# Router scores with the tokens as TensorE's held operand, and the norm's small term added in ScalarE's root

## The chip, the cores and the metric

The kernel runs on one core of a Trainium2 chip. The metric is the time of one execution on the device in microseconds, as the median of several runs. One more execution was recorded by the hardware profiler; all views below are of that one. The engines are PE (TensorE; PEld is its loading of the held operand), DVE (VectorE), ACT (ScalarE), POOL (GpSimd) and SP, which issues most of the transfers.

## What is computed

Two transformer blocks, one after the other, on 256 tokens of width 1024 in float32. Each ends its sublayers with a layer norm, and each has one sublayer of routed experts. The parts that the change touches are these:

```python
def _layer_norm(x, g, b):
    mu = jnp.mean(xf, axis=-1, keepdims=True)
    var = jnp.mean(jnp.square(xf - mu), axis=-1, keepdims=True)
    y = (xf - mu) * lax.rsqrt(var + LN_EPS) * g + b
...
def _grouped_moe(x, router_w, router_b, w1, w3, w2):   # first block, 16 experts
    scores = jax.nn.sigmoid((xt @ router_w).astype(jnp.float32))
    biased = scores + router_b.astype(jnp.float32)
    # two experts of one group per token, gates from scores, then the chosen experts
...
```

The second block has 8 experts of width 3584 and takes the two largest of `h @ moe_w_router` for each token; its gates are a softmax over these two.

## The kernel before

The tokens are kept as two tiles of 128 tokens (`TT = 2`), their width as eight blocks of 128 (`KT = 8`). `hT` holds the normed tokens turned round: width on the partitions, 256 tokens along the free axis. Every engine has one program, written out by hand, and semaphores tie them together. The work outside the experts is a list of units. TensorE emits a unit into a bank of PSUM (`emit`), ScalarE takes it out again (`save_unit`), and `proj_ready` and `proj_saved` count them. The bank is chosen by the unit's number, odd or even (`psB2` and `psB3`).

**The router.** After the norm ahead of it, TensorE turns the tokens (L1386, into `hT` by ScalarE at L1960), keeps itself busy with products that nobody reads (L1364), and then makes the scores by two units. Unit "held" (L1278) holds the router weights (16 or 8 columns) and moves all 256 tokens past them, eight products in all, one for each block of the width; ScalarE copies the result, experts on the partitions, to `route_rows` (L1979). Unit "back" (L1282) turns it round with two small transposes, and ScalarE saves it as scores with tokens on the partitions (L1981), through a sigmoid in the first block, which needs another table (ACT_TABLE_LOAD). VectorE then ranks and chooses (L2589 to L2602), TensorE counts the tokens of each expert with a triangular matrix (unit "cum", L1302), and VectorE turns the counts into places (L2622, L2608). In the first block a unit of 30 small products for a later stage ("compressed bias", L1325) stands on TensorE between the scores and the count. The experts' tokens are gathered (L1671), turned (L1687) and multiplied with weights that stream in by DMA (L1622; SP issues at L945). Their slots come free as the products use them.

**The norm.** VectorE sums the statistics (L2499), aggregates them to mean and variance in `mvar` (BN_AGGR, L2426), adds 1e-5 to the variance into `veps` (L2427), and asks ScalarE for the root (L1914). Then it takes the reciprocal (L2429) and scales the tokens (L2421). Seven norms do this once for each tile of 128 tokens (`norm_half`, on ScalarE `half_root`), two do it for both tiles at once (`layer_norm` with a source, L2443 to L2447, on ScalarE `root`, L1910). The last norm (L2410) has code of its own and isn't changed. `eps` is a column of the tile `small`, filled at the start.

Of the kernel before, what the change touches and what calls it, by code (L numbers as in the profile page):

```python
# [23 lines left out]
ALU = mybir.AluOpType  # L24
# [167 lines left out]
def two_block_kernel(nc, I, out):  # L192
    ctx = ExitStack()
    with ctx:
# [190 lines left out]
        rows_dram = nc.dram_tensor("bias_rows", (16, 2, ROW_W), F32, kind="Internal").ap()  # L385
        ones = sb("ones", [P, T])
        route = S[:].rearrange("p a b c -> p (a b c)")[:, 0:1000]
        route_rows = S[:].rearrange("p a b c -> p (a b c)")[:, 1024:1024 + T]
        at_slots = Slots(S[:].rearrange("p a b c -> p (a b c)")[:, 1280:1536], 0)
        slot_base, slot_id, gate_of, same_id = (at_slots.get(n) for n in (E2, TT * E2, TT * E2, TT * E2))  # L390
        two_back, back_gate, gate_sum = (at_slots.get(n) for n in (4, 4, TT))
# [218 lines left out]
        residual("mem1 out", I["mem_wo"][0])  # L610
        transposes("ln2 transposed", h, hT, 2)
        route_in = route[:, 0:TT * E1].rearrange("p (a b) -> p a b", a=TT)
        unit("router1", "held", (rw1, E1), route_rows[0:E1])
        unit("router1", "back", (E1,), route_in, ACT.Sigmoid)
        unit("compressed bias", "cb", (), bcmp)
        unit("count1", "cum", (route_gate[:, :, 0:E1], E1), route_count)
        routed("moe1")
# [5 lines left out]
        for i in range(2):  # L623
            transposes(f"ln{3 * i + 3} transposed", h, hT, 3 * i + 3)
            if i == 0:
                w = I["ev_w_in_2"][0]
                c = chunk(kxn(w)[:, :, 512:640], w=128)
                unit("mix2", "tok", (hT, c, KT, 128, 0, 128), ckv)
                c = chunk(kxn(w)[:, :, 1152:1224], w=72)
                unit("mix2", "dup", (hT, c, KT, 72, 0, 1), kiT)  # L630
                unit("mix2", "tok", (hT, c, KT, 72, 64, 8), wi, ACT.Copy, 8.0 ** -0.5)
                project("mix2", "T", hT, w, qiT, 640, 2)
                for j in range(8):
                    unit("indexer", "idx", (j,), idx_act[:, j % 2], ACT.Relu, 0.125)
                project("mix2b", "T", hT, w, qaT, 0, 2)
                project("mix2b", "T", hT, w, qbT, 1224, 2, scale=0.125)
                c = chunk(kxn(w)[:, :, 1736:1992])
                unit("mix2b", "dup", (hT, c, KT, 256, 0, 2), kbT)
                unit("mix2b", "tok", (hT, c, KT, 256, 128, 128), vb)
                for j in (0, 4, 1, 5):  # L640
                    unit("latent queries", "uk", (j,), qlatT[:, j:j + 3:2, :], ACT.Copy, 0.125)
                unit("latent keys", "ctr", (), cT)
                for j in range(4):
                    unit("latent out", "uv", (j,), yT[:, j, :])
                residual("out2", I["ev_w_out_2"][0])
            else:
                w = I["od_w_in_2"][0]
                project("mix3", "T", hT, w, kvcT[:, :, 0:T], 1024, 1)

                def queries(name, j, n):  # L650
                    project(name, "T", hT, w, qcT[:, 2 * j:2 * j + 2 * n, :], COLS * j, n, scale=0.125)

                for br, name in enumerate(("od_w1_k_2", "od_w1_v_2")):
                    if br == 1:
                        queries("mix3 first queries", 0, 1)
                        queries("mix3 second queries", 1, 1)
                    v = I[name][0].rearrange("(j d) c -> d j c", d=64)
                    cs = [chunk([(row, 64, 1024 * k, v[:, 16 * k + 8 * a:16 * k + 8 * a + 8, :]) for row in (0, 64)
                                 for k in range(2)], 16, 128) for a in range(2)]
                    unit(("compressed key parts", "compressed value parts")[br], "hidden", (br, cs), cmp_parts[:, br])  # L660
                c = chunk(kxn(w)[:, :, 1792:1840], w=48)
                unit("mix3 gates", "tok", (hT, c, KT, 48, 0, 48), g3, ACT.Sigmoid)
                own_banks()
                for g in range(2):
                    unit("compress joined", "join", (g,), geluT[:, :, g, 0:N_CMP], ACT.Gelu_apprx_tanh)
                queries("mix3 third queries", 2, 1)
                own_banks()
                unit("compress out", "kc", (), kcT)
                unit("compress out", "vc", (), vc4)
                queries("mix3 last queries", 3, 1)  # L670
                for c0, kd, vd in ((1280, ksT, vs), (1536, kwT, vw)):
                    c = chunk(kxn(w)[:, :, c0:c0 + 256])
                    unit("mix3 keys", "dup", (hT, c, KT, 256, 0, 2), kd)
                    unit("mix3 keys", "tok", (hT, c, KT, 256, 128, 128), vd)
                for t in range(TT):
                    adds.append(("compressed logits", None, t, None))
                for par in range(2):
                    unit("compressed probs", "pctr", (par,), pcT[:, par])
                residual("out3", I["od_w_out_2"][0])
            transposes(f"ln{3 * i + 4} transposed", h, hT, 3 * i + 4)  # L680
            project(f"xa{i} queries", "T", hT, I["xa_w_q_2"][i], mqT, 0, 2, scale=128.0 ** -0.5)
            residual(f"xa{i} out", I["xa_w_o_2"][i], 4)
            transposes(f"ln{3 * i + 5} transposed", h, hT, 3 * i + 5)
            if i == 0:
                experts("dense", FF_DENSE // COLS)
                in_part[0] = 3
            else:
                unit("router2", "held", (rw2, E2), route_rows[0:E2])
                unit("router2", "back", (E2,), route[:, 0:TT * E2].rearrange("p (a b) -> p a b", a=TT))
                unit("count2", "cum", (route_gate[:, :, 0:E2], E2), route_count[:, :, 0:E2])  # L690
                routed("moe2")

# [476 lines left out]
        def _(pe):  # L1169
# [35 lines left out]
            def turned_pair(u, k):  # L1205

                if u in behind_norm and k % 2 == 0:
                    pe.wait_ge(proj_saved, behind_norm[u] + 1 + k // 2)

            def emit(u):  # L1210
# [58 lines left out]
                elif kind == "tr":  # L1269
                    src, j0, _ = args  # L1270
                    for j in range(2):
                        for t in range(TT):
                            last = nc.tensor.transpose(bank[:, T * j + P * t:T * j + P * t + P],
                                                       src[:, t, P * (j0 + j):P * (j0 + j) + P], eye)
                elif kind == "held":
                    for k in range(KT):
                        turned_pair(u, k)
                        last = mm(bank[0:args[1], 0:T], args[0][:, k, :], hT[:, k, :], start=(k == 0), stop=(k == KT - 1))  # L1278
                elif kind == "back":
                    pe.wait_ge(proj_saved, u)  # L1280
                    for t in range(TT):
                        last = nc.tensor.transpose(bank[:, args[0] * t:args[0] * t + args[0]],  # L1282
                                                   route_rows[0:args[0], P * t:P * t + P], eye[0:args[0], 0:args[0]])
                elif kind == "ptr":
                    for k in range(2):
                        nc.tensor.transpose(bank[:, 32 * k:32 * k + 32], pe_rows[0:32, k], eye[0:32, 0:32])
# [608 lines left out]
        def _(act):  # L1895
# [11 lines left out]

            def root():
                request()
                answer(ap_(std, veps, ACT.Sqrt))  # L1910

            def half_root(t):
                request()
                answer(ap_(std[:, t:t + 1], veps[:, t:t + 1], ACT.Sqrt))  # L1914

            highs = [0]

# [35 lines left out]
            def save_unit(u):  # L1953
# [21 lines left out]
                        ins = ap_(dest, pair(bank), func, scale=scale)  # L1975
                    elif kind == "row":
                        ins = ap_(dest, bank[0:16, :], func)
                    elif kind == "held":
                        ins = ap_(dest, bank[0:args[1], 0:T], func)  # L1979
                    elif kind == "back":  # L1980
                        ins = ap_(dest, pair(bank, args[0]), func)  # L1981
                    elif kind == "cum":
                        ins = ap_(dest, pair(bank, args[1]), func, scale=scale)
                    elif kind == "sumsq":
# [352 lines left out]
        def _(dve):  # L2337
# [85 lines left out]

            def norm_half(t):

                do(V.bn_aggr(mvar[:, t, :], stats[:, t].rearrange("p a b -> p (a b)")))  # L2426
                ask(V.tensor_scalar(veps[:, t:t + 1], mvar[:, t, 1:2], EPS, None, ALU.add))  # L2427
                answer()
                do(V.reciprocal(rstd[:, t:t + 1], std[:, t:t + 1]))  # L2429
                for cut in (slice(0, D),) if t == 0 else (slice(0, D // 2), slice(D // 2, D)):  # L2430
                    scale_normed(h, t, cut)

            def layer_norm(src=None, ahead=None, stage=None, behind=None, alpha=None):
# [4 lines left out]
                if src is not None:  # L2438
                    for j in range(D // COLS):
                        ins = sums(src, j)  # L2440
                    do(ins)
                    for t in range(TT):
                        ins = V.bn_aggr(mvar[:, t, :], stats[:, t].rearrange("p a b -> p (a b)"))  # L2443
                    do(ins)
                    ask(V.tensor_scalar(veps, mvar[:, :, 1], EPS, None, ALU.add))
                    answer()
                    do(V.reciprocal(rstd, std))  # L2447
                    for t, cut in ((0, slice(0, D)), (1, slice(0, D // 2)), (1, slice(D // 2, D))):
                        scale_normed(src, t, cut)
# [739 lines left out]
```

## Time and profile before

| | us |
|---|---|
| median of 3 runs | 2262.59 (2260.28 to 2264.58) |
| the profiled execution | 2264.02 |
| its span, from first to last instruction | 2262.2 |
| busy in it: PE, DVE, ACT | 2141.7, 1551.9, 1274.8 |
| mean granted clock of TensorE, as a share of full speed | 0.97 |

The experts take the stretches from about 340 to 580 us and from about 1255 to 2240 us; the rest is attention and projections. In the timelines a row gives the start in us, the length in us, the engine, the line, what is written from what, the shapes, and in brackets for how long the engine had nothing to do and what ended that. A float32 product shows as two records, so eight products are x16. A row of stretches gives the busy time of each engine, then TensorE's granted clock (1.00 is 2.4 GHz, 0.50 is 1.2 GHz), the DMA engines' busy share and GB/s.

### The profile page before, as it was taken

The page shows a single profiled execution, that of the slowest core. Times are in us where ns is not written, and L with a number is a line of the kernel's source. Part 1 is how long each engine was busy: PE and PEld are TensorE (multiplying, and loading weights), DVE is VectorE, ACT ScalarE, POOL GpSimd, SP SyncE. Part 2 cuts the span into 40 slices and gives each one's busy share as a digit, 9 for nine tenths or more (in the row PEclk, how much of TensorE's full clock was granted, in tenths as well). Part 3 has the DMA queues.
Part 4 walks back from the last instruction along what each step waited for, and adds up shares of the span by engine and source line. Part 5 has one row for each costly group of instructions (what it writes and reads, how often), then busy time and mean ns, then how long its engine had stood idle before and what let it go on. Part 6 is the DMA issues. An engine that isn't in the chain of part 4 may idle for free. (4 is left out here: it accounts for less than half of the span.)

```text
span 2262.2 us, 33121 instructions
## 1 busy us (share of the span) xinstructions
PE 2141.7 (95%) x12242; PEld 1718.4 (76%) x12242; DVE 1551.9 (69%) x2217; ACT 1274.8 (56%) x1674; POOL 185.3 (8%) x142
## 2 busy tenths in 40 slices
PE   8998999998988989999999899999999999999996
PEld 8886884443787779997768688888888888888875
DVE  4557651221556686665377798898888888888987
ACT  4555441111334453443364777787777778777774
POOL 2112000000000013340000010001001010101000
PEclk9998998999989999998999899999999999999999
DMA  8640649999552244658212799999999999999994
GB/s 269 184 156 1 196 159 375 416 416 415 180 182 94 84 157 161 203 164 206 82 37 86 287 375 363 378 369 372 369 375 370 374 374 372 375 365 376 367 395 175
DMA packets 293952, 602.56 MB, mean 266 GB/s; under 512 B 17835, under 2 KB 123711, under 8 KB 285520
## 3 DMA queue, kind: packets, MB, share of 16 engines
q1 hardware_dynamic: 285392, 571.56, 69.8%
q0 software_dynamic: 8448, 29.49, 4.0%
q8 instruction: 72, 1.18, 0.2%
q14 instruction: 40, 0.33, 0.0%
HBM read 595.15 MB, written 5.83 MB: 266 GB/s over the span
## 5 line engine op out<-in xcount | busy, mean ns | idle before, releaser
L2099 ACT ACTIVATE arena_rounded<-ring 128x1024 fp32r<-128x1024 f32 x452 | 471.0, 1061 | 114.5 <-DMA ring<-in_moe_w_up_dram 65.0
L2810 DVE TENSOR_TENSOR ring_rounded<-ring,arena_rounded 128x1024 fp32r<-128x1024 f32 x452 | 525.2, 1218 | 12.8 <-ACT arena_rounded L2099 10.5
L1185 PE MATMUL psF<-arena_rounded 128*128 128x512 f32 x896 | 357.9, 399 | 1.5 <-ACT arena_rounded L2121 1.5
L1187 PE MATMUL psF<-arena_rounded 128*128 128x512 f32 x896 | 354.2, 395 | 0.0
L1186 PE MATMUL psF<-ring_rounded,arena_rounded 128*128 128x512 f32 x896 | 353.1, 394 | 0.0
L2371 DVE TENSOR_TENSOR ring_rounded<-ring,ring_rounded 128x2048 fp32r<-128x2048 f32 (+1 forms) x71 | 154.0, 2170 | 162.1 <-ACT ring_rounded L1925 161.9
L1187 PEld LDWEIGHTS psF<-arena_rounded 128*128 128x128 f32 x896 | 168.6, 188 | 39.3
L1185 PEld LDWEIGHTS psF<-arena_rounded 128*128 128x128 f32 x896 | 168.9, 188 | 38.9 <-ACT arena_rounded L2121 1.8
L1186 PEld LDWEIGHTS psF<-ring_rounded,arena_rounded 128*128 128x128 f32 x896 | 168.8, 188 | 37.9
L1186 PE MATMUL psB<-ring_rounded,PT_rounded 128*128 128x512 f32 x448 | 177.7, 397 | 0.0
L1925 ACT ACTIVATE ring_rounded<-ring 128x2048 fp32r<-128x2048 f32 (+1 forms) x71 | 128.6, 1813 | 84.7 <-PE psF L1187 62.7
L1185 PE MATMUL psB<-yT_rounded,ring_rounded 128*128 128x256 f32 x464 | 136.8, 295 | 5.3 <-DVE memT_rounded L2393 4.0
L2099 ACT ACTIVATE mv_rounded<-ring 128x1024 fp32r<-128x1024 f32 x110 | 116.7, 1061 | 38.1 <-DMA ring<-in_moe_w_down_dram 38.0
L1186 PE MATMUL psB<-memT_rounded,ring_rounded 128*128 128x256 f32 x464 | 135.3, 292 | 0.0
L1187 PE MATMUL psB<-yT_rounded,ring_rounded 128*128 128x256 f32 x464 | 135.0, 291 | 0.0
L2099 ACT ACTIVATE memT_rounded<-ring 128x1024 fp32r<-128x1024 f32 x110 | 116.1, 1062 | 31.3 <-DMA ring<-in_moe_w_down_dram 31.2
L2810 DVE TENSOR_TENSOR ring_rounded<-ring,memT_rounded 128x1024 fp32r<-128x1024 f32 x110 | 130.5, 1217 | 2.1 <-ACT memT_rounded L2099 1.4
L2810 DVE TENSOR_TENSOR ring_rounded<-ring,mv_rounded 128x1024 fp32r<-128x1024 f32 x110 | 129.3, 1216 | 0.0
L2815 DVE TENSOR_TENSOR PT_rounded<-psF,PT_rounded 128x512 fp32r<-128x512 f32 x56 | 38.7, 691 | 102.6 <-ACT PT_rounded L2109 102.6
L1187 PE MATMUL psB<-mv_rounded,PT_rounded 128*128 128x512 f32 x260 | 102.6, 395 | 0.0
L1187 PE MATMUL psF<-yT_rounded,ring_rounded 128*128 128x256 f32 x352 | 99.9, 284 | 0.0
L1185 PEld LDWEIGHTS psB<-yT_rounded,ring_rounded 128*128 128x128 f32 x464 | 93.2, 201 | 8.7 <-ACT hT L1960 5.8
(478 smaller groups left out, 4575.5 us busy)
## 6 DMA issues: line engine op xcount, KB each, us to landing
ring<-in_moe_w_gate_dram SPq DMA_DIRECT2D x224, 512.0 KB, 5.7
ring<-in_moe_w_up_dram SPq DMA_DIRECT2D x224, 512.0 KB, 5.7
ring<-in_moe_w_down_dram SPq DMA_DIRECT2D x224, 512.0 KB, 5.4
ring<-in_w_dram SPq DMA_DIRECT2D x48, 1024.0 KB, 16.4
arena<-in_w_dram SPq DMA_DIRECT2D x16, 1024.0 KB, 18.9
ring<-in_w_in_dram SPq DMA_DIRECT2D x14, 1024.0 KB, 5.3
ring<-in_ff_w_gate_dram SPq DMA_DIRECT2D x11, 1024.0 KB, 7.2
ring<-in_ff_w_up_dram SPq DMA_DIRECT2D x11, 1024.0 KB, 9.7
```

Source lines behind the costliest of these rows:

```text
L1185: mm(bank, x1, w1, start=start, stop=False, skip_group_check=open_groups)
L1186: mm(bank, x1, w2, start=False, stop=False, skip_group_check=open_groups)
L1187: return mm(bank, x2, w1, start=False, stop=stop, skip_group_check=open_groups)
L1925: ap_(ring_r[:, hi_slot[c], 0:kt * w].bitcast(R32), ring[:, slot_of[c], 0:kt * w], ACT.Copy)\
L2099: ap_(half_slot(slot, w_hi).bitcast(R32), half_slot(slot, raw_halves), ACT.Copy).then_inc(q["high"], 1)
L2371: V.tensor_tensor(ring_r[:, slot_of[c], 0:kt * w].bitcast(R32), raw, ring_r[:, hi_slot[c], 0:kt * w], ALU.subtract).then_inc(weights_low, 1)
L2810: V.tensor_tensor(half_slot(slot, low_halves).bitcast(R32), half_slot(slot, raw_halves), half_slot(slot, w_hi), ALU.subtract).then_inc(q[" ...
L2815: V.tensor_tensor(hiddenT_lo.bitcast(R32), Z[0][:, :].rearrange("p (f s) -> p f s", f=4), hiddenT_hi, ALU.subtract).then_inc(q["turned_dve ...
```

## The change

The two units of a router become one, "scores". It holds a block of the turned tokens (128 by 128) and moves the router weights (16 or 8 columns) past it: sixteen products, eight for each tile of tokens. The result has tokens on the partitions at once. The copy to `route_rows`, the transposes and their unit are gone. Since there is one unit less, all units between the two routers use the other one of the two banks; their order and waits are the same.

In nine norms the addition of 1e-5 on VectorE is gone (sixteen instructions: fourteen for a tile, two for both); ScalarE's root reads the variance from `mvar` and takes `eps` as its bias, and the aggregate is what asks for it.

```diff
-                elif kind == "held":
-                    for k in range(KT):
-                        turned_pair(u, k)
-                        last = mm(bank[0:args[1], 0:T], args[0][:, k, :], hT[:, k, :], start=(k == 0), stop=(k == KT - 1))
-                elif kind == "back":
-                    pe.wait_ge(proj_saved, u)
+                elif kind == "scores":
+                    w, n = args
                     for t in range(TT):
-                        last = nc.tensor.transpose(bank[:, args[0] * t:args[0] * t + args[0]],
-                                                   route_rows[0:args[0], P * t:P * t + P], eye[0:args[0], 0:args[0]])
+                        for k in range(KT):
+                            if t == 0:
+                                turned_pair(u, k)
+                            last = mm(bank[:, n * t:n * t + n], hT[:, k, P * t:P * t + P], w[:, k, :],
+                                      start=(k == 0), stop=(k == KT - 1))
...
             def half_root(t):
                 request()
-                answer(ap_(std[:, t:t + 1], veps[:, t:t + 1], ACT.Sqrt))
+                answer(ap_(std[:, t:t + 1], mvar[:, t, 1:2], ACT.Sqrt, bias=eps))
...
-                    elif kind == "held":
-                        ins = ap_(dest, bank[0:args[1], 0:T], func)
-                    elif kind == "back":
-                        ins = ap_(dest, pair(bank, args[0]), func)
+                    elif kind == "scores":
+                        ins = ap_(dest, pair(bank, args[1]), func)
...
             def norm_half(t):
 
-                do(V.bn_aggr(mvar[:, t, :], stats[:, t].rearrange("p a b -> p (a b)")))
-                ask(V.tensor_scalar(veps[:, t:t + 1], mvar[:, t, 1:2], EPS, None, ALU.add))
+                ask(V.bn_aggr(mvar[:, t, :], stats[:, t].rearrange("p a b -> p (a b)")))
                 answer()
```

TensorE at the first router, before. `hT` and `small` are the turned tokens and the router weights (here and below the router weights lie in `small`), `tab` and `ohot` are the later stage's bias.

```order
L1386 MATMUL psB<-cw,h 128x128 x8
L1364 MATMUL psF<-cw 128x256 x5
L1278 MATMUL psB<-hT,small 16x256 x8
L1282 MATMUL psB<-cw,S 128x16 x2
L1325 MATMUL psB<-tab,ohot 128x16 x30
L1302 MATMUL psB<-small,cw 128x16 x4
```

The same place after:

```order
L1382 MATMUL psB<-cw,h 128x128 x8
L1360 MATMUL psF<-cw 128x256 x5
L1278 MATMUL psB<-small,hT 128x16 x16
L1321 MATMUL psB<-tab,ohot 128x16 x30
L1298 MATMUL psB<-small,cw 128x16 x4
```

Eight products of 256 columns and two transposes have become sixteen products of 16 columns; the thirty bias products now stand right behind them.

ScalarE at the first router, before:

```order
L1960 ACTIVATE hT<-psB,small 128x256 x8
L1979 ACTIVATE S<-psB 16x256
L1981 ACT_TABLE_LOAD
L1981 ACTIVATE S<-psB 128x32
L2079 ACTIVATE arena<-h 128x2048
```

The same place after:

```order
L1956 ACTIVATE hT<-psB,small 128x256 x8
L1975 ACT_TABLE_LOAD
L1975 ACTIVATE S<-psB 128x32
L2073 ACTIVATE arena<-h 128x2048
L2076 ACTIVATE hT_rounded<-h 128x2048
```

The copy is gone, so the table load now follows the saves of the turned tokens directly.

## Rows read from the trace of the kernel before

**Rows 1.** the page, part 2: busy share of the DMA engines in 40 slices (tenths).
```profile
DMA  8640649999552244658212799999999999999994
```

**Rows 2.** the timeline around the first router: start us, length us, engine, line, what.
```profile
324.57 3.63 PE L1278 MATMUL psB<-hT,small 128*16 128x256 f32 x16
...
328.24 0.37 ACT L1979 ACTIVATE S<-psB 16x256 f32<-16x256 f32 x1 [2.63 <-PE psB L1278]
328.63 1.28 ACT L1981 ACT_TABLE_LOAD   x1
...
328.75 0.26 PE L1282 MATMUL psB<-cw,S 16*128 16x16 f32 x2 [0.55 <-ACT S L1979]
...
328.95 8.95 PE L1325 MATMUL psB<-tab,ohot 33*128 33x16 f32 x60
...
330.21 0.19 DVE L2643 TENSOR_TENSOR S<-S,small 128x32 f32<-128x32 f32 x1 [2.84 <-issue]
...
334.71 0.09 DVE L2602 MEMSET small<- 128x34 f32 x1
...
337.83 1.89 PE L1302 MATMUL psB<-small,cw 128*128 128x16 f32 x8
...
339.98 0.19 DVE L2622 TENSOR_TENSOR small<-small,S 128x32 f32<-128x32 f32 x1 [2.85 <-ACT small L1983]
```

**Rows 3.** the timeline around the second router.
```profile
1245.32 3.62 PE L1278 MATMUL psB<-hT,small 128*8 128x256 f32 x16
...
1248.97 0.37 ACT L1979 ACTIVATE S<-psB 8x256 f32<-8x256 f32 x1 [2.62 <-PE psB L1278]
...
1249.79 0.18 ACT L1981 ACTIVATE S<-psB 128x16 f32<-128x16 f32 x1 [0.44 <-PE psB L1282]
...
1250.07 0.29 DVE L2589 TENSOR_TENSOR S<-S 128x128 f32<-128x128 f32 x1 [1.96 <-ACT S L1981]
...
1252.08 0.38 PE L1302 MATMUL psB<-small,cw 128*128 128x8 f32 x1 [2.33 <-DVE small L2600]
```

**Rows 4.** the timeline of TensorE: two products in the form that the change takes.
```profile
80.32 3.63 PE L1259 MATMUL psB<-small,hT 128*128 128x4 f32 x32
...
646.03 3.74 PE L1259 MATMUL psB<-ring,hT 128*128 128x8 f32 x32
```

**Rows 5.** stretches: from:to us, length, each engine's busy us, TensorE clock, DMA share, GB/s.
```profile
84.23:87.64 3.41, 3.41 (x18) 3.41 (x17) 1.01 (x1) 0.00 (x0) 0.00 (x0) 0.50 0.35 119
328.95:333.40 4.45, 4.45 (x42) 4.45 (x40) 2.89 (x18) 4.44 (x4) 0.00 (x0) 1.00 1.02 428
333.41:353.88 20.47, 17.35 (x60) 12.06 (x61) 7.36 (x30) 4.34 (x10) 0.00 (x0) 0.50 0.85 351
351.00:354.00 3.00, 3.00 (x10) 1.06 (x8) 0.00 (x0) 0.00 (x0) 0.00 (x0) 0.52 0.02 8
400.00:450.00 50.00, 50.00 (x246) 20.79 (x244) 11.42 (x28) 7.15 (x12) 0.00 (x0) 1.00 1.02 417
650.84:654.25 3.41, 3.41 (x18) 3.41 (x18) 3.38 (x3) 0.00 (x0) 0.00 (x0) 0.50 0.96 284
```

**Rows 6.** the timeline of VectorE through the norm ahead of the second router.
```profile
1240.59 0.26 DVE L2426 BATCH_NORM_AGGREGATE small<-small 128x2 f32<-128x24 f32 x1
1240.89 0.15 DVE L2427 TENSOR_SCALAR small<-small 128x1 f32<-128x1 f32 x1
```

**Rows 7.** the same norm on ScalarE and TensorE, and VectorE in another norm.
```profile
1241.07 0.20 ACT L1914 ACTIVATE small<-small 128x1 f32<-128x1 f32 x1 [2.36 <-DVE small L2427]
...
1242.11 1.11 PE L1386 MATMUL psB<-cw,h 128*128 128x128 f32 x8 [0.34 <-DVE h L2421]
...
1194.93 0.42 DVE L2492 SCALAR_TENSOR_TENSOR h<-h,psF 128x256 f32<-128x256 f32 x1 [0.23 <-PE psF L1187]
```

**Rows 8.** groups by line: ns least/median/greatest, first and last start us; L2018 has a bias.
```profile
L2018 ACT ACTIVATE small<-small x8: 278/285/296, 718.6 to 727.7; 128x2 f32<-128x2 f32 x8
...
L2427 DVE TENSOR_SCALAR small<-small x14: 153/154/154, 244.9 to 1240.9; 128x1 f32<-128x1 f32 x14
```

More of the change, by code:

```diff
@@ L387, in two_block_kernel @@
         route = S[:].rearrange("p a b c -> p (a b c)")[:, 0:1000]
-        route_rows = S[:].rearrange("p a b c -> p (a b c)")[:, 1024:1024 + T]
         at_slots = Slots(S[:].rearrange("p a b c -> p (a b c)")[:, 1280:1536], 0)
@@ L612, in two_block_kernel @@
         route_in = route[:, 0:TT * E1].rearrange("p (a b) -> p a b", a=TT)
-        unit("router1", "held", (rw1, E1), route_rows[0:E1])
-        unit("router1", "back", (E1,), route_in, ACT.Sigmoid)
+        unit("router1", "scores", (rw1, E1), route_in, ACT.Sigmoid)
         unit("compressed bias", "cb", (), bcmp)
@@ L687, in two_block_kernel @@
             else:
-                unit("router2", "held", (rw2, E2), route_rows[0:E2])
-                unit("router2", "back", (E2,), route[:, 0:TT * E2].rearrange("p (a b) -> p a b", a=TT))
+                unit("router2", "scores", (rw2, E2), route[:, 0:TT * E2].rearrange("p (a b) -> p a b", a=TT))
                 unit("count2", "cum", (route_gate[:, :, 0:E2], E2), route_count[:, :, 0:E2])
@@ L1909, in root @@
                 request()
-                answer(ap_(std, veps, ACT.Sqrt))
+                answer(ap_(std, mvar[:, :, 1], ACT.Sqrt, bias=eps))
             def half_root(t):
                 request()
-                answer(ap_(std[:, t:t + 1], veps[:, t:t + 1], ACT.Sqrt))
+                answer(ap_(std[:, t:t + 1], mvar[:, t, 1:2], ACT.Sqrt, bias=eps))
             highs = [0]
@@ L2443, in layer_norm @@
                         ins = V.bn_aggr(mvar[:, t, :], stats[:, t].rearrange("p a b -> p (a b)"))
-                    do(ins)
-                    ask(V.tensor_scalar(veps, mvar[:, :, 1], EPS, None, ALU.add))
+                    ask(ins)
                     answer()
```

## The prediction, made before the change was run

> **What bounds the kernel now.** I read three kinds of view: the DMA engines over the whole span, then stretches with clock and DMA share, then the timelines at the places that the change touches. The DMA line of the page [rows 1] shows two long runs of 9 tenths, the two expert stages. In the first, the transfers run at 417 GB/s with a share of 1.02 (400 to 450 us [rows 5]): bandwidth bounds it. But from 351 to 354 us the share is 0.02 [rows 5]: all weight slots are full, and the stream waits until the first expert's products (L1622, from 348.56 us [rows 2]) free one. So what makes those products start earlier or later shifts the whole stage. The work ahead of it is a chain, and so is that ahead of the second expert stage.
>
> At the first router the chain is on TensorE: scores (324.57), transposes (328.75), thirty bias products (328.95 to 337.83), count (337.83) [rows 2]. VectorE has chosen its experts at 334.80 (L2602 [rows 2]), 3.0 us before the count starts, so it isn't late. At the second router no bias products stand in between: TensorE idled 2.33 us before the count, for VectorE (L2600) [rows 3]. There the chain runs scores, copy, transposes, save, VectorE.
>
> The stretches show one thing more. TensorE's clock is at its upper level (1.00, 2.4 GHz) through the first 4.45 us of the bias products and at 0.50 (1.2 GHz) from 333.41 to 353.88 us, though the engine was busy 4.45 of 4.45 us before it fell [rows 5]. What the engine did there was many products of few columns. The two other places with products of that kind [rows 4] are followed by such a fall too: products from 80.32, half clock from 84.23; products from 646.03, half clock from 650.84 [rows 4, 5]. The fall came 3.91, 4.81 and 4.45 us after the first narrow product.
>
> **The product itself.** Before: sixteen records, 3.63 and 3.62 us [rows 2, 3]. After: thirty-two records with a full 128 by 128 tile held each. That form stands in the trace: 3.63 us with 4 columns, 3.74 us with 8 [rows 4]. The bias products, of 16 columns, bound the wider one: 8.88 us for sixty records, 4.45 at full clock and 4.43 at half, is 4.45 + 2.21 = 6.66 us at full clock, 0.111 us a record, 3.6 us for thirty-two. The product costs 0 to 0.1 us more while the clock is up. The most it could cost is all of it at half clock: the count's eight records took 1.89 us there [rows 2], 0.236 each, 7.6 us for thirty-two.
>
> **First router.** Removed from TensorE: 0.55 us of waiting for the copy, and the transposes, so the bias products can start at about 328.3 instead of 328.95 (0.65 us less). The sigmoid's table load, 1.28 us [rows 2], now goes ahead of the wait for the product, and the scores come at 328.3 instead of 329.92; VectorE gains 1.6 us. That gain is worth nothing, because the count waits for the bias products, not for VectorE; without that cover it would be worth 1.6.
>
> Against this stands the clock. The narrow stretch now begins at 324.57, not at 328.95. With the middle lag, 4.4 us, the clock falls at 328.97: 0.67 of the 6.66 us of bias work is done by then, the other 5.99 takes twice as long, and the count starts at 328.97 + 11.98 = 340.95 instead of 337.83, 3.1 us later. The lags 3.91 and 4.81 give 3.6 and 2.7. If instead the clock fell where it does now, at 333.41, the work would be 5.11 + 2 x 1.55 us and the count would start at 336.5, 1.3 us earlier. Behind the count all is at half clock in both kernels until 353.88. The expert's wide products spend 5.32 us of that; if the clock comes back at the same instant, they spend 3.1 us less at half speed and half of the shift is given back (1.55 left); if it comes back after the same work, all of it stays. I take the middle of 1.55 and 3.1: **+2.3 us**. Bounds: -1.3 and, with a late return of the clock (rival 2), +4.8.
>
> **Second router.** Now 1.13 us pass from the end of the product (1248.94) to VectorE's first step (1250.07). After: ScalarE starts 0.03 us behind the product and VectorE 0.28 us behind ScalarE [rows 3], 0.31 in all, and the product is up to 0.12 longer. 1.13 - 0.31 - 0.12 = **-0.7 us**, and all of it is on the chain. The clock would fall at 1245.32 + 3.91 = 1249.2 at the earliest, behind the product's end at 1249.06. If it fell 1 us sooner, about 0.9 us of the product would double: +0.2 is the other bound.
>
> **The norms.** Fourteen additions of 0.15 us are gone [rows 8], and the two of the norms of both tiles. From the aggregate's end (1240.85) to the root's start (1241.07) there are 0.22 us now [rows 6, 7]; without the addition the root would start 0.03 us behind the aggregate, 0.19 earlier. But the root now takes a bias from memory. The trace has a column-sized activation with such a bias, L2018, 0.285 us [rows 8]; the root without one took 0.20 [rows 7]. That takes 0.08 back: 0.11 us a step. The Trainium skill, "ScalarE: Activation LUTs", section "What ACT_TABLE_LOAD costs", puts a pointer operand at about 93 ns more than an immediate; by that figure a step would gain 0.10. A root that is no dearer than now would gain 0.19. The row for L2018 stands with the former, so I leave the latter a bound: by it the norms would bring 1.8 us.
>
> How many steps count? In the norms behind both cross attentions and behind the dense layer, VectorE goes from one tile to the next without idling, and TensorE waits for it (0.34 us [rows 7]): six steps. In the four others the second tile's sum waits for TensorE (0.23 us [rows 7], L2492), so the first tile's gain is lost and the second's counts; in one of these, ahead of the first router, TensorE's filler products hold all but about 0.07. 9 x 0.11 + 0.07 = **-1.06 us**. The two norms of both tiles count nothing: VectorE next waits for ScalarE's halves of weights. Without that cover they would bring 0.11 each.
>
> **Sum.** +2.3 - 0.7 - 1.06 = +0.5 us. The profiled execution took 2264.02 us (span 2262.2), 1.4 above the median of the runs, 2262.59; the same shift on the median is 2263.1.
>
> **Rivals.**
> 1. *The clock doesn't fall earlier.* For it: the router's product keeps TensorE busy throughout, and its held tiles are full, which those of the bias products (33 rows) are not. Against: all three narrow stretches in the rows ended in a fall. The Trainium skill, "TensorE: Matmul & The Clock Gate", section "Why this matters for your kernels", ties a drop of the clock to gaps in which the engine idles; by that rule this change, which closes a gap, would keep the clock up longer. Price: -1.3 at the first router, -0.7, -1.06: -3.1 us, 2259.5.
> 2. *The return of the clock is late as well.* The mechanism is at the first expert, L1622. The clock came back 5.32 us after its first product. If, after the shift of 3.1, it stays down longer than that by as much as the shortest stretches at half clock in the rows last (3.41 us [rows 5]), 1.7 us of work is lost on top: +4.8. It decides at the point where a start of L1622 is too late for the return at 353.88 to hold; the products then start at 351.7 instead of 348.56, with 2.2 us left until then. Against: the fall may come later than I have it. With +0.2 at the second router and -1.06: +3.9 us, **slower**, 2266.5.
> 3. *The root's bias eats the norms' gain*, so that this half of the change doesn't do what it says. L2018's greatest is 0.296, which still leaves 0.1; the root isn't an exponential, though. Price: 0 instead of -1.06, 2264.2.
> 4. *The held tiles can't be loaded behind such short products*, or the product itself runs at half clock: 7.6 instead of 3.7 us, at both routers +7.8, 2271. The rows of the same form speak against it [rows 4].
>
> **Chances.** Forecast 0.50 (its own range 2261.0 to 2265.0), rival 1 0.22, rival 2 0.16, rival 3 0.08, rival 4 0.04. The range takes in rivals 1 to 3 and the spread of single runs, which was 2 us to either side: 2258.8 to 2266.8. A difference of 0.2% is 4.5 us, about what a measurement of this kernel can tell from none. Faster by more needs rival 1 with everything else at its good end, and some luck with the runs: 0.07. Slower by more needs rival 4, or rival 2 with some on top: 0.09. The same: 0.84.
>
> **What would show it.** Right: at the first router the scores' product takes 3.6 to 3.8 us; the clock is at 0.50 from about 329; the bias products take about 12.5 us instead of 8.9; the count starts near 341; the transfers resume 1.5 to 3 us later than now (after 354). At the second, VectorE's first step (L2589 before) is 0.7 us nearer to the start of the product; in the norms the root takes about 0.28 us and starts 0.03 behind the aggregate. Wrong: a clock that holds until 333 (rival 1), a stretch at half clock that is 3.4 us longer at its end (rival 2), a root of 0.4 us (rival 3), a product of 7 us (rival 4).

## The result and the profile after

The changed kernel took 2266.68 us (median of 20 runs, 2261.22 to 2273.94), the kernel before 2260.9 beside it (20 runs, 2255.07 to 2269.97): ratio 1.0024, 95% interval 1.0015 to 1.0033. By the ratio that is some 5.4 us slower (the two medians differ by 5.8) where +0.5 was forecast; the time lies 0.1 us inside the upper end of the range, 2266.8. The profiled execution has a span of 2266.1 us, against 2262.2 before.

The timeline of the changed kernel around the first router answers to [rows 2] (start us, length us, engine, line, what):

```profile
325.42 3.64 PE L1278 MATMUL psB<-small,hT 128*128 128x16 f32 x32
...
326.57 1.28 ACT L1975 ACT_TABLE_LOAD   x1
...
328.99 10.95 PE L1321 MATMUL psB<-tab,ohot 33*128 33x16 f32 x60
...
329.09 0.20 ACT L1975 ACTIVATE S<-psB 128x32 f32<-128x32 f32 x1 [1.24 <-PE psB L1278]
...
333.89 0.09 DVE L2594 MEMSET small<- 128x34 f32 x1
...
339.86 1.89 PE L1298 MATMUL psB<-small,cw 128*128 128x16 f32 x8
```

The product costs what it did (3.64 for 3.63 us). The bias products start 3.57 us behind the product's start, against 4.38 before, but they take 10.95 us for 8.95. VectorE has chosen its experts at 333.98, 5.9 us before the count starts. Counted from the product's start the count is at 14.4 us, against 13.3 before.

The stretches with clock and DMA share answer to [rows 5] (from:to us, length, each engine's busy us, TensorE clock, DMA share, GB/s):

```profile
328.99:331.19 2.20, 2.20 (x21) 2.20 (x20) 1.71 (x12) 2.10 (x3) 0.32 (x1) 1.00 1.01 428
331.20:355.10 23.90, 20.78 (x78) 16.08 (x79) 8.54 (x37) 5.72 (x10) 0.00 (x0) 0.50 0.87 360
353.00:356.00 3.00, 3.00 (x12) 1.09 (x10) 0.00 (x0) 0.00 (x0) 0.00 (x0) 0.64 0.01 3
```

The clock is up for 2.20 us of the bias products, where it was up for 4.45 in [rows 5], and is down to 355.10 instead of 353.88. The DMA engines stand still until the first expert frees a slot. SyncE's issues show when that is, first in the kernel before, then in the changed one:

```profile
354.85 4.24 SPq L945 DMA_DIRECT2D ring<-in_w_dram  x4
```

```profile
356.50 0.80 SPq L942 DMA_DIRECT2D ring<-in_w_dram  x2
```

At the second router and in the norm ahead of it, the timeline answers to [rows 3, 6, 7]:

```profile
1247.07 0.26 DVE L2420 BATCH_NORM_AGGREGATE small<-small 128x2 f32<-128x24 f32 x1
...
1247.37 0.29 ACT L1910 ACTIVATE small<-small 128x1 f32<-128x1 f32 x1 [2.17 <-DVE small L2420]
1247.69 0.16 DVE L2422 RECIPROCAL small<-small 128x1 f32<-128x1 f32 x1 [0.36 <-ACT small L1910]
...
1251.61 3.63 PE L1278 MATMUL psB<-small,hT 128*128 128x8 f32 x32
...
1255.28 0.18 ACT L1975 ACTIVATE S<-psB 128x16 f32<-128x16 f32 x1 [2.55 <-PE psB L1278]
...
1255.57 0.29 DVE L2581 TENSOR_TENSOR S<-S 128x128 f32<-128x128 f32 x1 [1.07 <-ACT S L1975]
...
1257.57 0.60 PE L1298 MATMUL psB<-small,cw 128*128 128x8 f32 x2 [2.33 <-DVE small L2592]
```

From the product's start to the count it is 5.96 us now against 6.76 in [rows 3]. The root takes 0.29 us with its bias against 0.20 in [rows 7] and starts 0.04 us behind the aggregate against 0.22.

So far nothing is worth 5 us. The rest stands where the forecast had no term at all, behind the first expert stage. There TensorE transposes the second memory input (mem2). First the kernel before, then the changed one:

```profile
580.20 0.68 DVE L2852 TENSOR_TENSOR arena<-arena,psF 128x512 f32<-128x512 f32 x1
...
581.49 3.74 PE L1273 MATMUL psB<-cw,yT 128*128 128x128 f32 x16 [1.37 <-DVE arena L2852]
```

```profile
582.45 0.69 DVE L2844 TENSOR_TENSOR arena<-arena,psF 128x512 f32<-128x512 f32 x1 [0.17 <-PE psF L1714]
...
586.95 3.74 PE L1270 MATMUL psB<-cw,yT 128*128 128x128 f32 x16 [4.54 <-issue]
```

In brackets is TensorE's idle time and what ended it. Before, it starts 0.6 us behind VectorE's last addition; now 3.8 us behind it, and "issue" says that the profile shows nothing it waited for. The DMA view of two short stretches tells more. The kernel before from 579 to 581.4 us, up to the transposes, has no packet of queue q8, and the next stretch, to 584, has one:

```profile
q1 hardware_dynamic: 543, 0.54, 68.9%
q14 instruction: 1, 0.01, 1.0%
```

```profile
q8 instruction: 1, 0.02, 2.3%
```

The changed kernel has one from 583.2 to 586.9 us, ahead of the transposes, and a second from 586.9 to 589:

```profile
q8 instruction: 1, 0.02, 1.9%
```

The packets of q8 are blocks of 16 KB of instructions (1.18 MB in 72 packets over the whole profile before). The profile doesn't name their engine; that they are TensorE's is concluded from who starts behind them.

### The profile page after: what moved, and what is told of

Read it like the earlier page. It is cut to its first block and busy times, and to the rows that moved or that the text cites. A ratio compares the mean times of both kernels' runs of the same rounds, so it can differ in the third digit from the quotient of the medians.

```text
span 2266.1 us, 33157 instructions
## 1 busy us (share of the span) xinstructions
PE 2144.3 (95%) x12270; PEld 1726.3 (76%) x12270; DVE 1549.5 (68%) x2201; ACT 1276.5 (56%) x1672; POOL 181.9 (8%) x142
## 5 line engine op out<-in xcount | busy, mean ns | idle before, releaser
L2802 DVE TENSOR_TENSOR ring_rounded<-ring,arena_rounded 128x1024 fp32r<-128x1024 f32 x452 | 525.6, 1219 | 14.4 <-ACT arena_rounded L2093 12.5
L1183 PEld LDWEIGHTS psB<-ring_rounded,PT_rounded 128*128 128x128 f32 x448 | 84.6, 189 | 19.6
```

The source lines that it names most:

```text
L1183: mm(bank, x1, w2, start=False, stop=False, skip_group_check=open_groups)
L2802: V.tensor_tensor(half_slot(slot, low_halves).bitcast(R32), half_slot(slot, raw_halves), half_slot(slot, w_hi), ALU.subtract).then_inc(q[" ...
```

## The experiments

Each run's time is compared with the kernel before on the same chip. The traces differ from one execution to the next, so this table collects what the profiled executions show, in us. "Fall" and "back" are the times after the product's start at which the clock goes to 0.50 and returns to 1.00; "loads" is when SyncE issues the first expert weights after the pause, also from the product's start; "gap" is from the end of VectorE's last addition of the first expert stage to the transposes of mem2, "norm" from there to the aggregate of the norm that follows.

| kernel | first router | count | fall, back | loads | gap | norm | ratio [95%] |
|---|---|---|---|---|---|---|---|
| before | held | 13.3 | 8.8, 29.3 | 30.3 | 0.6 | 14.3 | 1 |
| before again | held | 13.0 | 9.1, 19.3 | 26.2 | 0.6 | 14.6 | 0.9995 [0.9983, 1.0007] |
| norms alone | held | 16.0 | 5.8, 22.9 | 29.5 | 0.6 | 14.6 | 1.0013 [1.0002, 1.0024] |
| norms alone, again | held | 13.1 | 9.0, 29.5 | 30.3 | 0.6 | 14.3 | 1.0000 [0.9991, 1.0009] |
| before, 27 more | held | 13.5 | 8.6, 29.1 | 30.3 | 3.7 | 17.0 | 1.0018 [1.0008, 1.0028] |
| router 2 and norms | held | 13.0 | 9.1, 19.3 | 26.2 | 0.6 | 14.3 | 1.0000 [0.9991, 1.0009] |
| after | changed | 14.4 | 5.8, 29.7 | 31.1 | 3.8 | 17.2 | 1.0024 [1.0015, 1.0033] |
| after again | changed | 17.4 | 2.5, 33.2 | 34.3 | 3.6 | 17.0 | 1.0021 [1.0009, 1.0033] |
| routers alone | changed | 14.7 | 5.6, 29.5 | 31.1 | 4.1 | 17.3 | 1.0020 [1.0007, 1.0032] |
| after, 64 more | changed | 14.6 | 5.7, 29.6 | 31.1 | 0.6 | 14.4 | 1.0030 [1.0020, 1.0039] |
| after, 32 more | changed | 17.4 | 2.5, 33.3 | 34.3 | 0.7 | 14.4 | 1.0007 [0.9994, 1.0019] |
| after, filled | changed | 15.1 | 8.9, 22.6 | 28.7 | 4.1 | 17.5 | 1.0023 [1.0007, 1.0039] |

"Norm" counts from the last addition, so it holds the gap. Each kernel was profiled in one execution, while its ratio comes from 7 to 20 of its runs. The kernels with other work at these places, the two without the bias products, are told of below.

**Both kernels again, and each half of the change alone.** The halves are the edits of the change itself: the routers without the norms, and the norms without the routers.

> The kernel before once more, for how far one execution differs from another stage by stage. Theory A (the loss is made at the first router, by TensorE's clock falling earlier): the first router takes 13.3 us from the first score product to the count, as in the trace of before (13.26), whatever the other stages do; the stages with transfers (first experts, 340 to 595 us; second experts, 1252 to 2252 us) differ from the first trace of before by 1 to 3 us without any edit. Theory B (the expert stages or the swapped banks carry the loss): those stages repeat within 0.5 us, so that the +3.1 us seen there with the change is the change's.

> The changed kernel once more. Theory A: first router 14.4 us again, give or take 1 (it depends on the instant at which the clock falls: up to 16 us if it falls before the score product is done, 11.9 if it falls as late as before); first experts anything within 3 us of before. Theory B: the first expert stage again 3 us longer than before, and the stage from the second norm of both tiles to the end of the second attention again 2 us longer. Ratio against before 1.002 in both.

> Only the routers changed (one unit of sixteen narrow products each); the norms add their small term on VectorE as before. Theory A: all of the loss is here; first router 14.4 us, second router 0.8 us shorter than before; ratio 1.0025 to 1.003, a little above the full change's, since the norms' gain of about 1 us is missing. Rival (the root's bias costs more than it saves): ratio 1.000, like before.

> Only the norms changed (the root reads the variance and takes the small term as bias); the routers as before. Theory A: 0.10 us less from the aggregate to the reciprocal in each norm, in all -1.0 us; ratio 0.9995, not to be told from 1. Rival (the bias costs more): ratio 1.002.

Measured: see the table. The loss repeats (1.0021) and is in the routers' half (1.0020). The norms alone came out at 1.0013, against a trace in which the stretches with half norms are shorter as forecast. That contradiction was taken up with one more run:

> The kernel before with the norms' part of the change alone, once more. In its first run the trace showed 0.7 to 0.8 us less over the four half norms between the first output of the second layer and its last attention's, as forecast, and yet a ratio of 1.0013 [1.0002, 1.0024]. Theory (the norms give what the trace shows, and the first router's states of the clock, which cost 26.2 or 30.3 us of the same work from one execution to the next, spread the times): ratio 0.9996, within 0.9985 to 1.0007. Rival (the shorter norms shift the program against the clock so that the first router loses more often): ratio 1.001 again.

It gave 1.0000 [0.9991, 1.0009], so the rival isn't borne out. The first run's excess is not explained; its profiled execution had its fall at 5.8 us and its count at 16.0, which no other execution of the held form had.

**Where the code stands.** Behind the first expert stage TensorE's program has a branch: where no expert has too many tokens, it jumps over the code of a further round, and the transposes of mem2 stand at its target. Counted in the compiled program, TensorE's instructions at the first router are 27 more in the changed kernel: sixteen fp32 products are 64 (a weight load and a matmul, twice each), against 32 of the eight held ones and 4 of the two transposes; one wait is gone. All that follows on TensorE stands 27 instructions further on. The edit puts as many into the kernel before, at a place where TensorE waits anyway:

```
+            for _ in range(27):
+                pe.sem_inc(spaced, 1)
             pe.wait_ge(eye_in, 16)
             pe.wait_ge(mem_in, 16)
             run("mem1 transposed")
```

> The kernel before with 27 instructions more on TensorE at its start, where it waits for the identity anyway until 6.09 us: each only counts up a semaphore that nobody waits for. That is by how many instructions the changed kernel's TensorE program is longer at the first router (each fp32 product is a weight load and a matmul, twice over, each transpose one of each: 64 for 36, less one wait), so all that follows stands where it stands in the changed kernel. Theory placement: the 3 us that the changed kernel loses at the first transpose of mem2 (TensorE idle 4.54, 4.34 and 4.83 us ahead of it against 1.37, 1.34 and 1.33) come from where the code behind the first expert stage's branch stands: its start is not yet there and is fetched first. Then this kernel loses them too: idle about 4.5 us ahead of the transposes of mem2, an instruction fetch ahead of them instead of behind their start, ratio to the kernel before about 1.0014. Theory banks: the loss comes from the swapped result banks or from other waits of the changed program. Then this kernel is as the kernel before: idle 1.35 us, ratio 1.000. From the router's product to the restart of the expert weights' loads both expect 28.7 us (26.2 to 30.3 in three executions).

> The changed kernel with 64 instructions more on TensorE at its start, under the same wait for the identity. Theory placement: the code behind the first expert stage's branch stands elsewhere, 64 instructions further on, its start is there when the branch is taken, and TensorE is idle about 1.4 us ahead of the transposes of mem2 instead of 4.5: 3 us faster than the changed kernel, ratio to the kernel before about 1.0009. Theory banks: nothing changes, idle 4.5 us, ratio 1.0022. At the first router both expect what the changed kernel has: product to restart 31 to 34 us.

The kernel before, with nothing changed but these 27, now has the gap. The first row is it, the second the changed kernel with 64 more:

```profile
583.35 1.94 PE L1274 MATMUL psB<-cw,yT 128*128 128x128 f32 x8 [4.40 <-issue]
```

```profile
590.49 0.74 PE L1271 MATMUL psB<-cw,yT 128*128 128x128 f32 x5 [1.33 <-DVE arena L2847]
```

The one kernel got 3.1 us of gap and 1.0018, the other lost its gap. The second is nevertheless slower, 1.0030, and its start shows why: the first transposes begin at 10.74 us, where the identity is there at 6.09.

```profile
10.74 1.51 PE L1271 MATMUL psB<-cw,yT 128*128 128x128 f32 x6 [10.74 <-issue]
```

The spacers cost 4.65 us (0.0021); without them the ratio would be 1.0009, as expected. So with 32:

> The changed kernel with 32 instead of 64 counting instructions ahead of TensorE's first transpose. With 64 they took 0.154 us each and ran 4.65 us past the identity's arrival; 32 end within the 5.2 us of the wait. Theory placement: TensorE is idle 1.3 us ahead of the transposes of mem2, and the whole is 2.8 us faster than the changed kernel: what is left is the first router's +2.8, the second's -0.8 and the norms' -0.9, ratio to the kernel before 1.0005. Rival (64 instructions happened to help by something else, say the later start): idle 4.5 us, ratio 1.002.

```profile
584.47 0.69 DVE L2847 TENSOR_TENSOR arena<-arena,psF 128x512 f32<-128x512 f32 x1
...
585.85 0.45 PE L1271 MATMUL psB<-cw,yT 128*128 128x128 f32 x1 [1.42 <-DVE arena L2847]
```

No gap, and 1.0007 [0.9994, 1.0019] for the changed kernel's 1.0024. This is what the change does where the code happens to stand well. Banks and waits, the other theory, are the same in all three kernels and explain none of it. Over the executions of the table, the five with a gap (3.6 to 4.1 us) reach the next norm's aggregate after 17.2 us on average, the seven without after 14.4. The price of the placement is 2.8 us.

The packets of q8 tell the twelve apart. In the five with the gap one comes 1.1 to 1.6 us behind the last addition, and the transposes follow 2.5 to 3.0 us after it. In the seven without, none comes between the addition and the transposes: with 64 and 32 more, one had come 10.1 and 6.6 us ahead of the addition's end, and in the others the last one had come more than 22 us ahead.

**Without the bias products at the first router.** The same move in both kernels:

```
-            run("compressed bias")
             pe.wait_ge(chosen_ready, 1)
             run("count1")
             routed_layer(layers["moe1"])
+            run("compressed bias")
             pe.wait_ge(mem2_in, 16)
```

> The kernel before with the 30 products of the compressed bias (and ScalarE's save of them) moved out of the first router to behind the first expert stage. At the first router the count then waits for VectorE's choice of the experts, done 10.1 us after the product's start in the profile before: both theories expect the count at about 10.3 us after the product instead of 13.3, and the restart of the loads 3 us sooner. Behind the experts the 60 narrow matmuls cost up to 9 us. It stands here for the comparison with the next run. Theory bias products: what the changed router loses is that the bias products, started 0.04 us behind the scores' product instead of 4.4 us behind its start, run longer at the low clock and end later (10.95 us for 8.95), and that the count waits for them and not for the choice. Rival, clock alone: the wide products after the count run longer at the low clock whatever stands between.

> The same move in the changed kernel. Theory bias products: the changed router is now shorter than the other: the count starts 8.6 us after the product against 10.3 in the run before, so from product to restart about 1.7 us less; with 0.8 us at the second router and about 0.9 at the norms the whole is 3 us faster than the run before (ratio of the two about 0.9986), if the code behind the branch stands well in both. Rival, clock alone: the restart comes as late or later than in the run before although the count is sooner, and the whole is within 1 us of it or slower.

```profile
327.41 3.63 PE L1278 MATMUL psB<-hT,small 128*16 128x256 f32 x16
331.59 0.26 PE L1282 MATMUL psB<-cw,S 16*128 16x16 f32 x2 [0.56 <-ACT S L1979]
337.65 1.89 PE L1302 MATMUL psB<-small,cw 128*128 128x16 f32 x8 [5.80 <-DVE small L2600]
```

```profile
327.25 3.64 PE L1278 MATMUL psB<-small,hT 128*128 128x16 f32 x32
335.82 1.89 PE L1298 MATMUL psB<-small,cw 128*128 128x16 f32 x8 [4.93 <-DVE small L2592]
```

The count now waits for VectorE (in brackets) in both, 10.2 us after the product in the first and 8.6 in the second: the change is worth 1.7 us here as soon as the bias products don't hide it, as expected. The loads came 27.2 and 22.2 us after the product, 5.0 apart and not the 1.7 expected: the clock fell 9.0 and 5.9 us behind the product's start, but it also came back at 26.1 and 16.1. On the whole the two took 2271.32 and 2269.72 us (ratios to before 1.0043 [1.0027, 1.0059] and 1.0035 [1.0022, 1.0049]). The changed one is ahead by 1.6 us for 3 expected, within what seven runs each leave open. Both are slower than the kernels that they come from, since the sixty narrow records take 12.98 us at half clock behind the experts.

**What makes the clock fall earlier.** Wide work between the scores and the bias products:

```
             run("router1")
+            stay_warm(F[(add_span("mem1 out")[1] - 3) % 4], 4)
             run("compressed bias")
```

> The kernel of the run with 32, with 4 wide fp32 products (128 x 256, 1.9 us) between the scores' product and the bias products, and 16 counting instructions at the start for 32 (the 16 others are the fillers' own). Theory narrow product: the granted clock falls 5.7 us after the start of the changed product (8.6 to 9.1 in three of four executions of the held form), because the changed product moves 16 columns a matmul for 256 and TensorE's work is narrow from its start on, not only from the bias products on. With wide work behind it the fall comes later, 8.5 us or more after the product's start, and of the 1.9 us added a part comes back. Rival (the fall comes from the missing pause, or at a fixed time): the fall stays at 5.7 us, and the count starts 1.9 us later, 16.4 us after the product.

```profile
322.34:331.20 8.86, 8.86 (x72) 8.37 (x71) 7.24 (x31) 6.21 (x7) 0.70 (x1) 1.00 1.01 425
332.10:344.90 12.80, 11.02 (x42) 9.60 (x42) 4.27 (x20) 1.70 (x7) 0.00 (x0) 0.50 1.02 423
```

The clock held through the 8.86 us from the product's start on and fell at 8.9, where the five unfilled executions of the changed router had it at 2.5 to 5.8. The count came at 15.1 us in spite of 1.9 us of added work, the loads at 28.7 for 31.1 to 34.3. That is what the theory of the narrow product expected, but it is one execution. With the changed form and no fillers the fall came at 2.5 to 5.9 in six of six executions (the one without bias products among them); with the held form it came at 8.6 to 9.1 in six of seven and once at 5.8. That the changed form brings the fall forward rests on these thirteen; that wide work holds it back rests on one. The time of the kernel doesn't show the gain: 1.0023 [1.0007, 1.0039], with runs from 2257.69 to 2276.47 us. One reason stands in the trace, and it was not expected:

```profile
581.33 1.09 PE L1271 MATMUL psB<-cw,yT 128*128 128x128 f32 x4 [5.25 <-issue]
```

The gap is back, though counted in the compiled program the code behind the branch stands at the same place as in the kernel with 32 spacers (its 16 spacers and the 16 instructions of the fillers make 32 too). So placement alone doesn't decide. The packet of q8 that had come 6.6 us ahead of the last addition's end with 32 more comes 1.6 us behind it here; why it comes later stays open. Nor is the time explained by the gap: with the loads at 28.7 us, the gap's 2.8 us, and 1.8 us gained behind it (second router and norms), it would be about 1.0004, below the interval. The profiled execution took 2263.20 us, 3.4 less than the kernel's median, and may not stand for the others.

**The good parts alone.** First router as before, second router and norms as changed:

```
+        unit("router1", "held", (rw1, E1), route_rows[0:E1])
+        unit("router1", "back", (E1,), route_in, ACT.Sigmoid)
-        unit("router1", "scores", (rw1, E1), route_in, ACT.Sigmoid)
```

> The first router as before (weights held, turned back), the second router and the norms as changed. TensorE's program is the same as before up to the second router, so the placement behind the first expert stage is too. Theory (first router and placement are the whole loss): second router -0.8, norms -0.9, first router 26 to 30 us from product to restart as before, idle 1.35 us ahead of the transposes of mem2; ratio 0.9993. Rival (the norms' root or the second router costs elsewhere what it gives here): ratio 1.001, as the kernel with the norms alone had in its run.

No gap, the loads at 26.2 us, the second router at 5.96, and a ratio of 1.0000 [0.9991, 1.0009]. The forecast 0.9993 lies inside, and so does no gain. No kernel of this study beats the one before by more than its runs can tell.

## Why the prediction was right and where it failed

**Product.** Right: 3.64 and 3.63 us, rival 4 is out. (In the two executions whose clock fell after 2.5 us it took 4.6 and 4.5 us.)

**Second router.** Right: 5.96 or 5.97 us from product to count in seven of eight executions of the changed form (6.40 in the eighth, whose clock fell 3.0 us behind the product's start) for 6.76, so 0.8 us less where 0.7 was forecast.

**Norms.** Right in the trace: from the aggregate's start to the reciprocal's it is 0.62 us (1247.07 to 1247.69) instead of 0.72 (from [rows 6] to the reciprocal at 1241.31), so 0.10 a step where 0.11 was forecast, with a root of 0.29 us as the row of L2018 had it, and rival 3 is out. The reciprocal of before, on VectorE:

```profile
1241.31 0.17 DVE L2429 RECIPROCAL small<-small 128x1 f32<-128x1 f32 x1 [0.27 <-ACT small L1914]
```

The kernel with the norms alone shows in its times (1.0013, then 1.0000) neither this microsecond nor its absence. How many of the steps count, nine by the forecast, was not measured either: from the aggregate of the norm behind mem2 to the second router's product it takes 647.5 to 652.3 us, and these times overlap between kernels with and without the change.

**First router.** The mechanism was right: the narrow stretch begins earlier, so the clock falls earlier, the bias products run longer, and the count waits for them while VectorE's gain of 1.6 us is lost. The lag from the product's start to the fall was 5.8, 2.5, 5.6, 5.7 and 2.5 us, on average the 4.4 that the forecast took, but at two levels of which neither is 4.4. With a fall at 5.6 to 5.8 us the count moved by 1.2 to 1.4 us against the profile before, with one at 2.5 by 4.1 (3.1 forecast); the bias products took 11.0 to 11.2 and 13.0 us (12.5 forecast). Mis-sized is the term. Over six executions of the held form the loads resume 28.8 us after the product (26.2 to 30.3), over five of the changed one without fillers 32.4 (31.1 to 34.3): **+3.6 us**, for +2.3 forecast and inside its bounds. The step that failed is the sum against one execution. Against that one, with 30.3, the five stand at +2.1, close to the forecast; but two of the six of the held form had their clock back after 19.3 us and the loads at 26.2, and no execution of the changed form came under 31. With so few executions and such spreads, +3.6 may be off by 1 us or more either way (an estimate from the spread of these eleven).

Rival 2 came near in its time and not in its mechanism. In two of five executions the clock came back 33.2 and 33.3 us behind the product's start, and the loads at 34.3, 4.0 us over the profile before (4.8 priced). But the rival wanted a clock that stays down longer than 5.32 us behind the first expert's first product, which starts here in the kernel before:

```profile
348.56 8.85 PE L1622 MATMUL psF<-ring,arena 128*64 128x512 f32 x28 [0.83 <-issue]
```

In the five executions of the changed form it stayed down 4.1 to 5.2 us behind that product. What made two of them late was the fall at 2.5 us, earlier than any lag in the forecast: their count already stood 4.1 us later.

**The missing term.** The prediction took work as all that moves, and went from the restart of the loads to the second router with a shift of 1 to 1. From the restart to the last addition of the experts that held within the spread of the executions (227.0 us on average over the six of the held form, 226.6 over the five). At the branch behind them it didn't: **+2.8 us** for code that stands 27 instructions further on. No rival had it, so it is luck that the range holds the time: without these 2.8 us the kernel would lie well inside it, at 2263.9, and the range was made wide for other reasons. The Trainium skill, "Runtime: NRT & Kernel Launch", section "Instruction fetch mechanics", says that a taken branch whose target lies outside what has been fetched makes the engine wait for that block. The gap of 3.8 us with a 16 KB packet in it agrees with that, and so do the seven executions without gap, which have no packet there. What the rule alone doesn't tell is in which kernel the block has been fetched in time: the one with 32 more and the filled one differ in it.

**Sum of what was found.** +3.6 + 2.8 - 0.8 - 1.0 = +4.6 us, for 5.4 measured (3.4 to 7.5) and 4.7 in the repeat. Taken up to the experts' last addition in place of the loads, the first term is +3.1 and the sum +4.1. For the other kernels the same terms give 1.0025 for the routers alone (1.0020 measured), 1.0012 for before with 27 more (1.0018), 1.0029 for after with 64 more, their 4.65 us included (1.0030), and 1.0008 for after with 32 more (1.0007), each inside its interval, though the terms come from these kernels' own traces; the filled kernel (1.0004 for 1.0023 measured) is the one that they don't explain; the norms alone (0.9996) lie inside the second of their two (1.0002 to 1.0024, then 0.9991 to 1.0009). By a threshold of 0.2% the ratio falls to "slower", to which the forecast had given 0.09 ("the same" had 0.84), though its interval begins below that threshold, at 1.0015.

## What to carry to other kernels

When TensorE's program changes length, look at every branch behind the change: an idle time "issue" ahead of the first instruction behind it, with a packet of an instruction queue in it, points to a cost of placement, and a few idle instructions at a place where the engine waits tell it from the cost of the change. Before a term is sized against one execution, look at more executions of the same kernel for that stretch, when a clock or another thing with levels takes part in it. A matmul form that is equal in time need not be equal in what happens to the clock behind it: here the narrow form took 3.64 us for 3.63, and the products that followed paid for it.

## What the runs showed of the hardware that was not expected

- The start of the code behind a branch cost 2.8 us or nothing by 27 instructions of distance (1.0018 [1.0008, 1.0028] for 27 idle instructions more), and once cost it at a place where another kernel had it free.
- Counting a semaphore up costs TensorE about 0.15 us each: 64 of them ran from 0.84 to 10.53 us.
- The granted clock fell while TensorE was busy without a gap: in the changed kernel for all of the 11.20 us ahead of 331.20. In the one execution with 1.9 us of wide products put in, at a place that had no gap to close, the fall came 8.9 us behind the product's start for at most 5.8. The Trainium skill, "TensorE: Matmul & The Clock Gate", section "Why this matters for your kernels", ties drops to idle gaps. Here it fell under an engine that was busy, and it fell earlier with the narrow form, which closes a gap of 0.55 us, than with the held one; the measurement decides.
- Of the same work at the first router, the executions of one kernel show two costs, 26.2 or 30.3 us before the loads resume (31.1 or 34.3 in the changed kernel), and the traces differ there in when the clock falls and returns.
